# A two-block transformer kernel on one core: block 2's memory products moved into block 1's layer norms, its position table made by one product, its mixer's norm factor applied at the projections' evictions

## The chip, the core and the metric

The kernel runs on one core of a Trainium2 chip. Its time is the device time of one execution, in microseconds (us), and the number that counts is the median over the runs. The engines are TensorE (PE in the profile), VectorE (DVE), ScalarE (ACT), GpSimd (POOL) and SyncE (SP), which here only issues transfers. Each engine goes through its own instructions in order and waits on semaphores for the others.

## The reference, cut to what matters

Sequence 256, width 1024. Block 1 has two layers, each a hybrid mixer, a layer norm, a feed-forward part (dense SwiGLU in layer 0, eight experts in layer 1) and a layer norm. Block 2 has one layer, and only it changes:

```python
x = x + 0.5 * swiglu_ffn(rms_norm(x, ffn1_norm), ...)            # FFN 1
h = rms_norm(x, mix_norm)
q_a, k_a, v_a, q_i, k_i, w_i, u_s, q_m, gates = split(h @ w_in)  # 19 projections
bias = rel_bias[t5_bucket(sel - t)]                              # 32 buckets, 8 heads
mem_kv = rms_norm(mem, mem_norm) @ w_mem_kv                      # 256x1024 @ 1024x512
m_k, m_v = split(mem_kv)
... sparse attention, S5 states, memory attention, gates, w_out, FFN 2
```

`mem` is an input of its own: `mem_kv` and the position table depend on nothing that block 1 computes. An RMS factor is one number per token (row), so it may be applied after a product with the weights as well as before.

## The kernel before

Everything is one program, written out in order for each engine (blocks for `sync`, `gpsimd`, `tensor`, `scalar`, `vector`); no scheduler moves anything. The stages follow each other: mixer 0, layer norm 0, dense FFN, layer norm 1, mixer 1, layer norm 2, router and experts, layer norm 3, FFN 1 of block 2, preparation for block 2's mixer, that mixer, FFN 2.

**The ring.** All weights pass through a ring of six 1 MB places in SBUF (`ring_data`, class `Ring`, L155). SP issues load n in two halves as soon as PE has finished with n + 1 - 6 loads, which it tells by the semaphore `weights_used` (L170). The loads are numbered in the order of use: per mixer 14 projections and four parts of `w_out` (`MIX_LOADS` = 18), per dense FFN 33, then the experts.

**Split weights.** In the FFNs and experts each weight load is split by ACT (`high`, `e_high`: a rounded copy) and DVE (`low`, `e_low`: what is left), and PE multiplies the parts. At the end of each mixer, ACT and DVE split the first two loads of what comes next; on DVE these two come ahead of the residual adds (L2390 to 2398), and on ACT ahead of the norm's square root.

**A layer norm stretch.** After the last product of a mixer, DVE makes four residual adds with statistics (L2398), ACT a square root, DVE four normalizing operations, PE turns x (L889), and ACT and DVE evict it. PE has nothing else to do in between.

**Preparation (L1375 to L1400 of PE).** After FFN 1 PE turns the normalized memory (L874), multiplies it with `w_mem_kv` (two loads, L1384, 32 products 256 wide), makes the position table head by head (L1391: eight products 512 wide with the head's bias row repeated over 128 columns, each evicted by ACT and stored to DRAM by POOL), turns the S5 blocks (L1397, L1398), and turns the normalized x (L874), which ACT and DVE evict with `mix_norm`. Then the 19 projections start (L1413 to L1424). DVE normalizes x between (L2579), ACT squares it. The squares and the scaling of `mem` itself run in FFN 1 on ACT and DVE.

Of the kernel before, what the change touches and what calls it, by code (L numbers as in the profile page):

```python
# [10 lines left out]
ALU = mybir.AluOpType  # L11
# [38 lines left out]
FFN_LOADS, MOE_LOADS = 3 * FFN_CHUNKS, 3 * MOE_CHUNKS  # L50
LEVELS = 6
# [11 lines left out]
N_MEM = N_FFN1 + FFN_LOADS  # L63
N_PROJ2 = N_MEM + 2
# [6 lines left out]
R2_LDT, R2_FFN1, R2_MIX, R2_MEM, R2_FFN2, R2_LRE, R2_LIM, R2_D, ROWS2 = 0, 8, 16, 24, 32, 40, 48, 56, 58  # L71
# [49 lines left out]
def constant_offsets():  # L121
# [9 lines left out]
    ("lambda_inverse", "mk_sumsq", "mk_normed", "heads_sumsq", "heads_normed", "keys_chosen", "states_ready"),  # L131
    ("relb_ready", "angle_reduced", "blocks_ready", "powers_ready"),
    ("dt_ready", "unit_act", "mk_std", "mkT_act", "heads_std", "ys_ready"),
    ("router_psum", "place_psum", "bc_psum", "mkT_psum", "y_psum"),
# [113 lines left out]
PARAMS = {"pcol": (DEPTH, P), "hpar": (DEPTH, 24), "nrmw": (DEPTH, HD), "cln": (DEPTH, 2, CW), "router": (DT, E)}  # L248
# [6 lines left out]
def small_parameters(v):  # L255
# [13 lines left out]
    parts.append(v["moe_router"][0].reshape(DT, P, E).transpose(1, 0, 2).reshape(P, DT * E))  # L269
    return np.ascontiguousarray(np.concatenate(parts, 1), dtype=np.float32)  # L270
# [7 lines left out]
def two_block_kernel(nc, a, out):  # L278

    CO, CONST_W = constant_offsets()  # L280
    with ExitStack() as ctx:
# [59 lines left out]
        pcol, hpar, nrmw, cln, router_sb = (param(k) for k in PARAMS)  # L341
# [66 lines left out]
        sq, forget = ar(6, T), ar(T)  # L408
        fs, fp, fpT = ([ar(3 * P) for _ in range(2)] for _ in range(3))
        kend, vb = ar(TT, GW), ar(TT, GW)  # L410
        norm12, beta1, beta2, qscale, qsquare = ar(TT, 2 * H), ar(TT, H), ar(TT, H), ar(TT, H), ar(TT, H)
# [45 lines left out]
        ring2 = Ring(ring_data, [sem(f"loaded2_{i}") for i in range(RING)], sem("weights2_used"), sem("weights2_hi"), sem("weights2_lo"), (2 * MIX_LOADS + FFN_LOADS) % RING)  # L457
# [7 lines left out]
        tstage = bu.rearrange("p a b c -> p (a b c)").rearrange("p (h c) -> p h c", h=AH)  # L465
# [11 lines left out]
        qiT, kiT, kaT = ar(2, T), ar(T), ar(T)  # L477
        kva, kd = ar(TT, P), ar(TT, P)
        uT = ar(2, T)
        mkT = ar(2, T)  # L480
        at_bT = ar.at
        bT, cT = ar(2, 2, P), ar(2, 2, P)
        mkv = cln.rearrange("p a b c -> p (a b c)").rearrange("p (j c) -> p j c", j=TT)
        over = Area(at_q)
        relb, relb_bc = over(AH), over(AH, P)
# [5 lines left out]
        memx = arena[:, at_pw:at_pw + TT * D].rearrange("p (j d) -> p j d", j=TT)  # L491
        squares = arena[:, at_bT:at_bT + D]
        mk_sq = arena[:, 3 * D * TT:3 * D * TT + TT * T].rearrange("p (j c) -> p j c", j=TT)
        memT = arena[:, 4096:6144].rearrange("p (k t) -> p k t", k=DT)
# [4 lines left out]
        hi2 = [h[:, i, :] for h in (hi_gates, hi_bu) for i in range(3)]  # L499
        bufs2 = ffn_buffers(2, at_bu + 3 * 8 * FC, cln.rearrange("p a b c -> p (a b c)").rearrange("p (s j c) -> p s j c", s=2, j=TT))  # L500
# [4 lines left out]
        row1, row2 = sm(TT), sm(TT)  # L505
# [41 lines left out]
        n_moe = 2 * MIX_LOADS + FFN_LOADS  # L547
        dense_banks = [[4, 5], [6, 7]], [[0, 1], [2, 3]]
        ffn = Gated(sem, "ffn", ring, hi1, lo_slots, MIX_LOADS, 0, FFN_CHUNKS, 0, *dense_banks, (xT_hi, xT1_lo), bufs1)
# [16 lines left out]
        T_FFN, T_FFN1, T_MEM, T_MIX, T_MERGED, T_FFN2 = 2, 6, 7, 8, 9, 10  # L566
        SPLIT, MIXED = (T_FFN, T_FFN1, T_FFN2), (1, 4)

# [11 lines left out]
        def _(sp):  # L580
            sp.dma_start(actT[:, :, :], a["xT"]).then_inc(sem("xT_loaded"), 16)

            def mixer(l):
                n0 = (MIX_LOADS + FFN_LOADS) * l
                for m, (c, w, _) in enumerate(PROJ):
                    ring.load(sp, n0 + m, ring.slot(n0 + m)[:, 0:8 * w].rearrange("p (k c) -> p k c", k=DT), cols(a["w_in"][l], c, w))
                for m in range(OUT_LOADS):
                    n = n0 + len(PROJ) + m
                    ring.load(sp, n, ring.slot(n).rearrange("p (k c) -> p k c", k=DT), cols(a["w_out"][l], FC * m, FC))
# [269 lines left out]
        def _(pe):  # L859
# [41 lines left out]
            def mixer(l):  # L901
# [256 lines left out]
                for m in range(OUT_LOADS):  # L1158
                    out(m, (5, 6, 7), last=True)
# [1657 lines left out]
```

## Time and profile before

| what | us |
|---|---|
| runs before | 2364.22, 2367.36, 2368.49; median 2367.36 |
| span of the profiled execution | 2365.2 |
| PE busy in it | 2264.0 (96%) |
| end of FFN 1 to first projection of block 2 | 1861.6 to 1895.2 |
| layer norm 0, 1, 2 (PE's last product before to first product after) | 202.3 to 212.0, 404.9 to 415.8, 606.0 to 616.9 |

For the profiled execution only its span is given, from its first to its last instruction; it lies 2.2 us under the median of the runs. In a timeline row stand the start, the duration (from the first to the last of the instructions merged), engine, line, operation, tiles, count, and in brackets how long the engine stood idle before and what released it. A product of f32 stands in the trace as two instructions, a transpose as one.

### The profile page before, as it was taken

Reading aid. Unit: us, or ns where it says so; the run is one execution under the profiler, and the core shown is the slowest. Engines: PE = TensorE matmul, PEld = TensorE weight load, DVE = VectorE, ACT = ScalarE, POOL = GpSimd, SP = SyncE. Lnnn points to the kernel's source line nnn. Section 1 sums busy time; section 2 is a strip of 40 time slices with the busy share of each in tenths; the row PEclk is TensorE's granted clock in tenths of the full one; section 3 lists DMA queues with packets and bytes.
Section 4 is the critical chain, followed back from the end, with each engine's and each line's share of the span. In section 5 each row is a group of like instructions: output and inputs, shape, how many; then the busy total and the mean of one; then the engine's idle time right before and its main releaser. Section 6 shows DMA issues by size and latency. Waiting matters only on the chain.

```text
span 2365.2 us, 31984 instructions
## 1 busy us (share of the span) xinstructions
PE 2264.0 (96%) x12197; PEld 1864.0 (79%) x12197; DVE 1538.5 (65%) x1675; ACT 1159.3 (49%) x1159; POOL 146.1 (6%) x226
## 2 busy tenths in 40 slices
PE   8988998999799999999999999998899999999998
PEld 7977886887678888888888888886688788758886
DVE  3646444473688989898888989897655219434443
ACT  3133442313366777677677767676545211214442
POOL 1100000210200000000000000000570001000000
PEclk9999999999799999999999999999899999789999
DMA  8224554421489999999999999999355444224552
GB/s 288 71 75 143 180 188 152 125 78 54 144 328 347 357 341 356 354 352 358 343 357 344 353 344 354 345 355 329 120 200 180 153 148 128 89 89 134 180 189 75
DMA packets 254773, 538.02 MB, mean 227 GB/s; under 512 B 17839, under 2 KB 146913, under 8 KB 254433
## 3 DMA queue, kind: packets, MB, share of 16 engines
q1 hardware_dynamic: 250960, 523.21, 63.1%
q0 software_dynamic: 3168, 9.86, 1.3%
q10 hardware_dynamic: 560, 3.79, 0.4%
q8 instruction: 58, 0.95, 0.2%
q14 instruction: 27, 0.21, 0.0%
HBM read 533.65 MB, written 3.15 MB: 227 GB/s over the span
## 4 chain that ended last, share of the span: by engine, by line
PE 92%; DVE 5%; ACT 1%; issue 1%; DMA 0%; DVEq 0%; SPq 0%; ACTq 0%
PE bank L1290 9%; PE bank L1289 9%; PE bank L1293 9%; PE bank L1164 8%; PE bank L1165 8%; PE bank L1166 8%; PE bank L920 5%; PE bank L1424 5%; PE bank L1309 4%; PE bank L1304 4%; PE bank L1305 4%; PE bank L1111 2%; PE bank L1264 1%; DVE arena L2278 1%; PE bank L1572 1%; PE bank L1277 1%
## 5 line engine op out<-in xcount | busy, mean ns | idle before, releaser
L2082 DVE TENSOR_TENSOR weights_lo<-ring_data,weights_hi 128x2048 fp32r<-128x2048 f32 x336 | 759.6, 2290 | 101.3 <-ACT weights_hi L1813 100.2
L1813 ACT ACTIVATE weights_hi<-ring_data 128x2048 fp32r<-128x2048 f32 x336 | 637.4, 1917 | 177.5 <-DMA ring_data<-in_moe_w 176.3
L1289 PE MATMUL bank<-weights_hi,xg_hi 128*128 128x512 f32 x896 | 357.2, 399 | 4.0 <-DVE arena L2483 2.6
L1290 PE MATMUL bank<-weights_hi,xg_lo 128*128 128x512 f32 x896 | 354.6, 396 | 0.0
L2077 DVE TENSOR_TENSOR weights_lo<-ring_data,weights_hi 128x2048 fp32r<-128x2048 f32 x99 | 229.3, 2345 | 56.3 <-ACT weights_hi L1622 56.3
L1293 PE MATMUL bank<-weights_lo,xg_hi 128*128 128x512 f32 x896 | 242.9, 393 | 0.0
L1597 ACT ACTIVATE arena<-bank 128x384 f32<-128x384 f32 (+5 forms) x152 | 74.8, 514 | 335.7 <-PE bank L1424 99.0
L1164 PE MATMUL bank<-weights_hi,xT_hi 128*128 128x512 f32 x528 | 213.3, 404 | 2.3 <-DVE xT_lo L2070 2.3
L1165 PE MATMUL bank<-weights_lo,xT_hi 128*128 128x512 f32 x528 | 209.7, 397 | 0.0
L1166 PE MATMUL bank<-weights_hi,xT_lo 128*128 128x512 f32 x528 | 209.3, 396 | 0.0
L1289 PEld LDWEIGHTS bank<-weights_hi,xg_hi 128*128 128x128 f32 x896 | 168.2, 188 | 42.9 <-issue 3.0
L1293 PEld LDWEIGHTS bank<-weights_lo,xg_hi 128*128 128x128 f32 x896 | 168.4, 188 | 40.1
L1290 PEld LDWEIGHTS bank<-weights_hi,xg_lo 128*128 128x128 f32 x896 | 168.7, 188 | 38.8
L1622 ACT ACTIVATE weights_hi<-ring_data 128x2048 fp32r<-128x2048 f32 x99 | 185.7, 1918 | 0.0
L1304 PE MATMUL bank<-weights_hi,hT_hi 128*128 128x512 f32 x448 | 177.8, 397 | 1.5 <-DVE hT_lo L2489 1.5
L1305 PE MATMUL bank<-weights_hi,hT_lo 128*128 128x512 f32 x448 | 175.7, 392 | 0.0
L920 PE MATMUL bank<-actT,ring_data 128*128 128x256 f32 x608 | 136.1, 383 | 0.0
L2098 DVE TENSOR_TENSOR hT_lo<-bank,hT_hi 128x256 fp32r<-128x256 f32 x66 | 25.0, 420 | 170.2 <-ACT hT_hi L1633 170.2
L1633 ACT ACTIVATE hT_hi<-bank 128x256 fp32r<-128x256 f32 x66 | 21.7, 381 | 219.3 <-PE bank L1185 219.3
L920 PEld LDWEIGHTS bank<-actT,ring_data 128*128 128x128 f32 x608 | 115.3, 191 | 16.8 <-issue 0.4
L1309 PE MATMUL bank<-weights_lo,hT_hi 128*128 128x512 f32 x448 | 123.1, 397 | 0.0
L1164 PEld LDWEIGHTS bank<-weights_hi,xT_hi 128*128 128x128 f32 x528 | 100.1, 190 | 25.6 <-DVE xT_lo L2070 2.9
(444 smaller groups left out, 3198.4 us busy)
## 6 DMA issues: line engine op xcount, KB each, us to landing
ring_data<-in_moe_w SPq DMA_DIRECT2D x672, 512.0 KB, 4.4
ring_data<-in_ffn_w_in SPq DMA_DIRECT2D x88, 512.0 KB, 4.7
ring_data<-in_w_in SPq DMA_DIRECT2D x70, 512.0 KB, 4.8
ring_data<-in_ffn_w SPq DMA_DIRECT2D x66, 512.0 KB, 4.1
ring_data<-in_ffn_w_out SPq DMA_DIRECT2D x44, 512.0 KB, 4.0
ring_data<-in_w_out SPq DMA_DIRECT2D x24, 512.0 KB, 4.4
ring_data<-in_w_in SPq DMA_DIRECT2D x8, 396.0 KB, 4.1
ring_data<-in_w_in SPq DMA_DIRECT2D x8, 390.0 KB, 5.4
```

The lines of the kernel that those rows point to most:

```text
L920: i = mm(bk(b, 2, T)[:, g], wt[:, k, P * g:P * g + P], actT[:, k, :], start=k == 0, stop=k == DT - 1)
L1164: mm(o, x_hi, w_hi, start=start, stop=False, **kw)
L1165: mm(o, x_hi, w_lo, start=False, stop=False, **kw)
L1166: return mm(o, x_lo, w_hi, start=False, stop=stop, **kw)
L1289: mm(o, xg_hi[:, k, :], e_hi(at)[:, r], start=k == 0, stop=False)
L1290: mm(o, xg_lo[:, k, :], e_hi(at)[:, r], start=False, stop=False)
L1293: i = mm(bank[2 * part + q][:, :], xg_hi[:, k, :], e_lo(at)[:, r], start=False, stop=k == DT - 1)
L1304: mm(o, ehT_hi[:, 2 * m + f, :], w_hi[:, f, cd], start=first and f == 0, stop=False)
L1305: mm(o, ehT_lo[:, 2 * m + f, :], w_hi[:, f, cd], start=False, stop=False)
L1813: nc.scalar.activation(e_hi(at), ring_data[:, e_slot(at), :], ACT.Copy).then_inc(ring.hi_done, 1)
L2077: v.tensor_tensor(f.lo_slot(f.n0 + at), w, f.hi_slot(f.n0 + at), ALU.subtract).then_inc(f.ring.lo_done, 1)
L2082: v.tensor_tensor(e_lo(at), ring_data[:, e_slot(at), :], e_hi(at), ALU.subtract).then_inc(ring.lo_done, 1)
```

## The change

- `w_mem_kv` is loaded in four quarters of 128 columns (0.5 MB each), each in a place of block 1's ring: one between mixer 0 and the dense FFN, one between that and mixer 1, two between mixer 1 and the experts. PE multiplies a quarter (`memory`: 16 products 128 wide) after the last product of mixer 0, of the dense FFN and of mixer 1, and after the router's product. ACT evicts each with the memory's RMS factor.
- `mem` comes in twice in the first microseconds, once as it is (for the squares) and once transposed by the host (`memT`), on ACT's queue behind `x`; ACT scales `memT` by `mem_norm` (eight copies) and squares `mem` (two) in mixer 0. Nothing of it is left in FFN 1.
- The position table comes from one product (8 x 512) ahead of layer norm 3's transposes, evicted once, and stored by one transfer that reads the eight rows 128 times.
- PE turns x itself after FFN 1, ACT and DVE evict it with `mix_norm`, and the row factor is applied at the evictions: per token tile on ACT (two instructions where one was), and for the three products that stand transposed by DVE, with the factors spread over the partitions by two small products (`spread_rows`). The S5 blocks are turned after the second projection.

Core of the diff:

```diff
+N_MIX = (0, MIX_LOADS + 1 + FFN_LOADS + 1)
+N_FFN = MIX_LOADS + 1
+N_KV = (MIX_LOADS, N_MIX[1] - 1, N_MIX[1] + MIX_LOADS, N_MIX[1] + MIX_LOADS + 1)
+N_MOE = N_KV[3] + 1
# SP
             mixer(0)
+            memory(0)
             dense(ffn, a["ffn_w1"][0], a["ffn_w3"][0], a["ffn_w2"][0])
+            memory(1)
             mixer(1)
+            memory(2)
+            memory(3)
# POOL
-            pool.dma_start(memx[:, :, :], a["mem_2"][0].rearrange("(j p) d -> p j d", p=P)).then_inc(sem("mem_loaded"), 16)
-            for h in range(AH):
-                pool.wait_ge(sem("toep_act"), h + 1)
-                pool.dma_start(toep[h], tstage[:, h, :]).then_inc(sem("toep_stored"), 16)
+            pool.wait_ge(sem("act_stage"), stage("toep_act"))
+            pool.dma_start(toep, bc(tstage[0:AH, :], 1, P)).then_inc(sem("toep_stored"), 16)
+            pool.wait_ge(sem("toep_stored"), 16)
+            pool.wait_ge(sem("x_fed"), TT)
# PE
+            def memory(u, b):
+                n = N_KV[u]
+                ring.arrived(pe, n)
+                if u == 0:
+                    pe.wait_ge(sem("mem_scaled"), DT)
+                wt = ring.slot(n)[:, 0:8 * P].rearrange("p (k c) -> p k c", k=DT)
+                for j in range(TT):
+                    for k in range(DT):
+                        i = mm(bk(b, TT, P)[:, j], memT[:, k, P * j:P * j + P], wt[:, k, :], start=k == 0, stop=k == DT - 1)
+                i.then_inc(ring.used, 1)
...
                 for m in range(OUT_LOADS):
                     out(m, (5, 6, 7), last=True)
+                memory(2 * l, 7)
                 transpose_halves(x, 2 * l)
...
                 i.then_inc(sem("pe_stage"), 1)
+                memory(3, 6)
                 pe.wait_ge(sem("sel_ready"), 1)
...
+                mm(bank[5][0:AH, :], relb[0:32, :], const("hot")[0:32, :], start=True, stop=True).then_inc(sem("pe_stage"), 1)
...
-                for m in range(3):
-                    project(m)
+                project(0)
+                spread_rows()
+                project(1)
+                turn_blocks()
+                project(2)
# ACT
+                    if l == 0 and m == 1:
+                        act.wait_ge(sem("mem_loaded"), 32)
+                        for k in range(DT):
+                            a_(memT[:, k, :], memT[:, k, :], ACT.Copy, "mem_scaled", scale=memg[:, k:k + 1])
...
+                act.wait_ge(sem("pe_stage"), stage("toep_psum"))
+                a_(tstage[0:AH, :], bank[5][0:AH, :], ACT.Copy, "act_stage")
...
+                    for j in range(TT):
+                        a_(dst[:, j], o[:, j], f, "proj2_act" if j == TT - 1 else "act_steps", scale=rowm[:, j:j + 1])
# DVE
-            xT_out(T_MEM, gain(R2_MEM), memT, (4, 5, 6, 7))
-            rms(2, x, hbuf)
-            prepare_more()
-            xT_out(T_MIX, gain(R2_MIX))
-            keys_norm()
+            xT_out(T_MIX, gain(R2_MIX), actT, (4, 5, 6, 7))
+            mixer_factor()
+            keys_norm()
+            dve.wait_ge(sem("act_stage"), stage("row_spread"))
+            projected(0)
+            projected(1)
+            prepare_more()
```

SP's queue where mixer 0 ends and the dense FFN begins, and where mixer 1 ends and the experts begin (L184 and L187 are the same line of `Ring.load`; x8 of `w_out` are the halves of four loads). Before:

```order
L184 DMA ring_data<-in_w_in 128x4x256 x6
L184 DMA ring_data<-in_w_out 128x4x256 x8
L184 DMA ring_data<-in_ffn_w 128x4x256 x4
...
L184 DMA ring_data<-in_w_in 128x4x256 x6
L184 DMA ring_data<-in_w_out 128x4x256 x8
L646 DMA ring_data<-in_moe_w 128x1024 x16
```

And now:

```order
L187 DMA ring_data<-in_w_in 128x4x256 x6
L187 DMA ring_data<-in_w_out 128x4x256 x8
L187 DMA ring_data<-in_w_mem_kv 128x4x128 x2
L187 DMA ring_data<-in_ffn_w 128x4x256 x4
...
L187 DMA ring_data<-in_w_in 128x4x256 x6
L187 DMA ring_data<-in_w_out 128x4x256 x8
L187 DMA ring_data<-in_w_mem_kv 128x4x128 x4
L670 DMA ring_data<-in_moe_w 128x1024 x16
```

One load of memory weights stands ahead of the dense FFN's first, two ahead of the experts' first.

PE where mixer 1 ends, layer norm 2 and the router (before: L1111 is `w_out`, L889 turns x, L1246 is the router, L1250 to L1254 rank the tokens, L1264 gathers):

```order
L1111 MATMUL bank<-ring_data,actT 128x256 x24
L889 MATMUL bank<-consts_sb,x 128x128 x16
L1246 MATMUL bank<-params,actT 128x8 x16
L1250 MATMUL bank<-small,consts_sb 128x8
L1251 MATMUL bank<-small,consts_sb 128x8
```

And now (L1141, L905, L1279, L1284, L1285 are the same lines; L926 is `memory`):

```order
L1141 MATMUL bank<-ring_data,actT 128x256 x24
L926 MATMUL bank<-ring_data,arena 128x128 x16
L905 MATMUL bank<-consts_sb,x 128x128 x16
L1279 MATMUL bank<-params,actT 128x8 x16
L926 MATMUL bank<-ring_data,arena 128x128 x16
L1284 MATMUL bank<-small,consts_sb 128x8
L1285 MATMUL bank<-small,consts_sb 128x8
```

A quarter stands ahead of the turn of x, another between the router and the ranking.

PE from FFN 1's end to the third projection, before:

```order
L874 MATMUL bank<-consts_sb,arena 128x128 x16
L1384 MATMUL bank<-ring_data,arena 128x256 x32
L1391 MATMUL bank<-consts_sb,arena 128x512 x8
L1397 MATMUL bank<-consts_sb,arena 128x128
L1398 MATMUL bank<-consts_sb,arena 128x128
...
L874 MATMUL bank<-consts_sb,lnp 128x128 x16
L1413 MATMUL bank<-actT,ring_data 128x256 x16
L1417 MATMUL bank<-actT,ring_data 64x256 x16
L1420 MATMUL bank<-ring_data,actT 128x4 x16
L1424 MATMUL bank<-ring_data,actT 128x256 x16
```

And now:

```order
L890 MATMUL bank<-consts_sb,x 128x128 x16
L1438 MATMUL bank<-actT,ring_data 128x256 x16
L1414 MATMUL bank<-consts_sb,small 128x128 x2
L1442 MATMUL bank<-actT,ring_data 64x256 x16
L1445 MATMUL bank<-ring_data,actT 128x4 x16
L1422 MATMUL bank<-consts_sb,arena 128x128
L1423 MATMUL bank<-consts_sb,arena 128x128
...
L1449 MATMUL bank<-ring_data,actT 128x256 x16
```

The turn of the memory, its products and the table are gone from here; the two spreading products and the turn of the blocks stand behind the first and the second projection.

## Rows read from the trace of the kernel before

**Rows 1.** The page: the span, and the chain that ended last by engine.
```profile
span 2365.2 us, 31984 instructions
...
PE 92%; DVE 5%; ACT 1%; issue 1%; DMA 0%; DVEq 0%; SPq 0%; ACTq 0%
```

**Rows 2.** Timeline of PE from FFN 1's end to the first projection.
```profile
1861.62 1.91 PE L874 MATMUL bank<-consts_sb,arena 128*128 128x128 f32 x16
1864.89 14.05 PE L1384 MATMUL bank<-ring_data,arena 128*128 128x256 f32 x64 [1.36 <-ACT arena L1597]
1878.88 9.24 PE L1391 MATMUL bank<-consts_sb,arena 32*128 32x512 f32 x16
...
1890.56 3.62 PE L874 MATMUL bank<-consts_sb,lnp 128*128 128x128 f32 x16
1895.20 7.14 PE L1413 MATMUL bank<-actT,ring_data 128*128 128x256 f32 x32 [1.02 <-ACT actT L1597]
```

**Rows 3.** Timeline of DVE, end of block 2's states.
```profile
2040.71 0.87 DVE L2700 SCALAR_TENSOR_TENSOR arena<-arena,params,bank 128x256 f32<-128x256 f32 x2 [13.49 <-PE bank L1475]
```

**Rows 4.** Timeline of DVE at the end of mixer 0 and of mixer 1.
```profile
197.86 0.68 DVE L2398 SCALAR_TENSOR_TENSOR x<-x,bank 128x512 f32<-128x512 f32 x1
...
202.34 0.69 DVE L2398 SCALAR_TENSOR_TENSOR x<-x,bank 128x512 f32<-128x512 f32 x1 [0.26 <-PE bank L1111]
...
597.12 4.49 DVE L2082 TENSOR_TENSOR weights_lo<-ring_data,weights_hi 128x2048 fp32r<-128x2048 f32 x2 [1.97 <-ACT weights_hi L1813]
601.53 0.68 DVE L2398 SCALAR_TENSOR_TENSOR x<-x,bank 128x512 f32<-128x512 f32 x1
```

**Rows 5.** SP's queue: the loads released by the parts of `w_out`.
```profile
194.74 0.94 SPq L184 DMA_DIRECT2D ring_data<-in_ffn_w  x2
598.23 0.81 SPq L646 DMA_DIRECT2D ring_data<-in_moe_w  x2
600.82 0.80 SPq L646 DMA_DIRECT2D ring_data<-in_moe_w  x2
```

**Rows 6.** Timeline: PE leaves a place (experts' first load); ACT waits for its next content.
```profile
640.16 1.07 PE L1293 MATMUL bank<-weights_lo,xg_hi 128*128 128x512 f32 x4
646.02 1.92 ACT L1813 ACTIVATE weights_hi<-ring_data 128x2048 fp32r<-128x2048 f32 x1 [1.39 <-DMA ring_data<-in_moe_w]
```

**Rows 7.** Timeline of PE, layer norm 2 to the gather.
```profile
616.91 6.96 PE L1246 MATMUL bank<-params,actT 128*128 128x8 f32 x32 [0.88 <-DVE actT L2057]
626.07 0.60 PE L1250 MATMUL bank<-small,consts_sb 128*128 128x8 f32 x2 [2.19 <-DVE small L2424]
631.25 5.54 PE L1264 MATMUL bank<-arena,x 128*128 128x128 f32 x32 [2.88 <-DVE arena L2458]
```

**Rows 8.** The chain: products after layer norm 1; a gather among the experts.
```profile
415.79 7.58 PE bank L918 x32
...
747.58 3.57 PE bank L1264 x32
```

**Rows 9.** The table by stretch: PE, PEld, DVE, ACT, POOL busy (count), granted clock, DMA share, GB/s.
```profile
405.00:410.00 5.00, 0.00 (x0) 0.00 (x0) 4.59 (x11) 0.20 (x1) 0.00 (x0) 0.96 0.40 107
416.00:420.00 4.00, 4.00 (x13) 4.00 (x14) 0.00 (x1) 0.00 (x0) 0.00 (x0) 0.53 0.46 152
1880.00:1890.00 10.00, 9.31 (x20) 3.57 (x20) 0.00 (x0) 4.78 (x8) 4.38 (x8) 0.71 0.82 288
```

**Rows 10.** Timeline of ACT ahead of FFN 1 (layer norm 3).
```profile
1666.34 0.21 ACT L1597 ACTIVATE small<-params 128x8 f32<-128x8 f32 x1 [4.86 <-DVE params L2593]
1666.45 3.01 ACT L1597 ACTIVATE xT_hi<-bank,params 128x256 fp32r<-128x256 f32 x8
```

**Rows 11.** Timeline of DVE in mixer 0, where it waits for PE.
```profile
64.46 0.56 DVE L2239 TENSOR_TENSOR arena<-bank,small 128x384 f32<-128x384 f32 x1 [3.84 <-PE bank L972]
```

**Rows 12.** The table by stretch (columns as in rows 9), mixer 0.
```profile
45.00:50.00 5.00, 5.00 (x25) 4.41 (x24) 0.78 (x2) 2.80 (x8) 0.00 (x0) 1.00 0.08 9
```

**Rows 13.** Groups of POOL's instructions, 1855 to 1990 us: busy, mean ns | idle before.
```profile
L841 POOL DMA_DIRECT2D toep<-arena x8 | 4.4, 547 | 126.0 <-ACT arena L1597 126.0
```

More of the change, by code:

```diff
@@ L589, in mixer, with memory @@
                     ring.load(sp, n, ring.slot(n).rearrange("p (k c) -> p k c", k=DT), cols(a["w_out"][l], FC * m, FC))
+            def memory(u):
+                n = N_KV[u]
+                ring.load(sp, n, ring.slot(n)[:, 0:8 * P].rearrange("p (k c) -> p k c", k=DT), cols(a["w_mem_kv_2"][0], P * u, P))
             def up(f, w1, w3, c, at, r):
@@ L667, in _ @@
             dense(ffn1, w[:, 0:FFN], w[:, FFN:2 * FFN], a["ffn1_w_out_2"][0])
-            for m in range(2):
-                ring2.load(sp, N_MEM + m, slots_of(N_MEM + m, DT), cols(a["w_mem_kv_2"][0], FC * m, FC))
             for m, (c, w, _) in enumerate(PROJ2):
@@ L1576, in _ @@
             dense(ffn, 0)
+            memory(1, 7)
             transpose_halves(x, 1)
@@ L1668, in norm_std, with memory_out @@
                 a_(std[:, 0:TT], mv[:, :, 1], ACT.Sqrt, "ln_std", bias=LN_EPS)
+            def memory_out(u, b):
+                act.wait_ge(ring.used, N_KV[u] + 1)
+                if u == 0:
+                    act.wait_ge(sem("dve_stage"), stage("mem_factor"))
+                for j in range(TT):
+                    a_(mkv[:, j, P * u:P * u + P], bk(b, TT, P)[:, j], ACT.Copy, "mem_kv", scale=mem_r[:, j:j + 1])
             def mixer(l):
-                n0 = (MIX_LOADS + FFN_LOADS) * l
+                n0 = N_MIX[l]
                 def project(m):
@@ L1730, in mixer @@
                     a_(sq[:, 2 * m:2 * m + 2, :], qkv[:, 2 * m:2 * m + 2, :], ACT.Square, "qk_squares")
+                if l == 0:
+                    for j in range(TT):
+                        a_(memsq, memx[:, j, :], ACT.Square, "act_stage", accum_out=mem_ss[:, j:j + 1])
+                        act.wait_ge(sem("act_stage"), stage("mem_sq0") + j)
                 project(5)
@@ L1734, in mixer @@
                 act.wait_ge(sem("gdn_psum"), 7 * l + 6)
+                if l == 0:
+                    a_(mem_r[:, :], mem_ss[:, :], ACT.Sqrt, "act_stage", scale=1.0 / D, bias=NORM_EPS)
                 a_(norm12[:, :, :], bk(2, TT, 2 * H), ACT.Sqrt, "gdn_act", bias=NORM_EPS)
@@ L1950, in branches @@
                 a_(mkT[:, :, :], bk(4, 2, T), ACT.Copy, "act_stage")
-                for m in range(3, 7):
+                for m in (3, 4, 6):
                     project(m)
@@ L2021, in _ @@
             norm_std(1)
+            memory_out(1, 7)
             xT_out(3)
@@ L2215, in mixer @@
                 dve.wait_ge(sem("gdn_act"), 7 * l + 6)
+                if l == 0:
+                    dve.wait_ge(sem("act_stage"), stage("mem_std"))
+                    v.reciprocal(mem_r[:, :], mem_r[:, :]).then_inc(sem("dve_stage"), 1)
                 st.do(v.reciprocal(norm12[:, :, :], norm12[:, :, :]))
```

201 lines of the change are left out of this document (94 added, 107 removed).

## Prediction

> **What bounds the kernel now.** I read the chain of waits first: 92% of it is PE, and DVE, ACT and the rest share 8% [rows 1]. So only what PE itself does, or what it stands still for, counts. Then I went through PE's timeline for the two kinds of place that the diff touches. Between FFN 1 and block 2's first projection PE is nearly always busy, with work that needs nothing from block 1: it turns the memory from 1861.62, multiplies it for 14.05 us from 1864.89, makes the position table for 9.24 us from 1878.88, turns the blocks and x, and only at 1895.20 starts projecting [rows 2]. In the layer norm stretches PE stands still and DVE is the chain. Last I read who releases DVE there: its first residual add starts straight behind the split of the next stage's first two loads (4.49 us for two, 601.53 behind them), and only the fourth waits, 0.26 us, for PE [rows 4]. So DVE has no slack at the ends of the mixers, and that decides much below.
>
> **Part 1: the preparation leaves PE's path.** What is left between FFN 1 and the first projection is one turn of x and its eviction. The same steps stand in the trace as the turn of the memory: sixteen transposes from 1861.62, the evictions, the next product at 1864.89 [rows 2]. That its second half must now wait for the last add into x changes little, since x is added while PE still multiplies; I take 1865.0. Against 1895.20 that is -30.2 us. Two things come back: the blocks' eight transposes (sixteen took 1.91 us at one clock and 3.62 at the other [rows 2], so 0.9 to 1.8, and 0.9 amid full-speed projections) and the two spreading products (four instructions of 128 columns; 32 took 3.57 [rows 8], so 0.45). With a gap or so 1.5 us. Net -28.7. Bounds: if both run slow and PE waits for an eviction here and there, -26; if nothing comes back, -30.2. The row factor: ACT has two instructions for each projection where it had one, DVE three more, but each projection keeps PE for some 7 us (7.14 [rows 2]), and PE asks for a bank only four projections later. The factor itself (square, root, reciprocal, spreading) runs beside the first projection. DVE's chain of states has 13.49 us in which it waits at its end [rows 3], so a start a microsecond later costs nothing.
>
> **Part 2: the ring loses places at the mixers' ends.** The four quarters are loads of the ring. With six places, load n starts when PE is through with load n - 5. Before, the dense FFN's first two loads were numbers 18 and 19 and hung on the uses 13 and 14 of mixer 0, projections both; the third hung on the first part of `w_out`, and that one was issued at 194.74 [rows 5]. Now a memory quarter is 18, so the FFN's second load is number 20 and hangs on the first part of `w_out`: it will be issued at 194.74. Before the experts two quarters stand, so both of their first loads wait, for the first and second parts: 598.23 and 600.82 [rows 5], where now two later loads start. How long from release to ACT's split? Among the experts PE leaves a place at 641.23 (640.16 + 1.07) and ACT starts on its next content at 646.02, having waited for the DMA: 4.8 us [rows 6].
> Mixer 0: ACT splits at 194.74 + about 4.8 = 199.6, rounded up to 199.8 for the longer `ffn` rows, ends 1.92 later [rows 6] at 201.7, DVE takes 2.25 (half of 4.49 [rows 4]) to 204.0, and only then starts the adds, which started at 197.86. The fourth add stood 4.48 behind the first, with 0.26 of waiting that is now gone: 208.2 against 202.34. **+5.8.**
> Mixer 1: the second load is issued at 600.82; ACT starts at 605.6 and ends at 607.5, DVE at 609.8 against 601.53. Less the 0.26 [rows 4], **+8.0.** Bounds of the two together: +11 if loads land in 3.5 us, +17 if each meets another transfer.
>
> **Part 3: the products themselves.** A quarter is 16 products of 128 columns, 32 instructions, like the gather: 3.57 us warm [rows 8]. Behind mixer 0, the dense FFN and mixer 1 PE stands idle for longer than that, in the first and third now for longer still: 0. The fourth stands between the router and the ranking. There the granted clock is the lower level: the gather of the same 32 instructions took 5.54 [rows 7], since the clock rose only on its way. PE is free at 623.87 (616.91 + 6.96) and is asked for the ranking at 626.07 [rows 7]: 5.5 us of product put that off by 3.3. If the clock is then up, the ten ranking instructions take half (about -1.1) and the gather 3.57 for 5.54 (-2.0). Sum **+0.3**; bounds +4.7 (6.9 us at 1.2 GHz as the router's 32 instructions, nothing won) and -1.
> Layer norm 1 is where the filled gap may pay. Before, PE was idle from 404.9, the granted clock read 0.96 over 405 to 410 and 0.53 over 416 to 420 [rows 9]: it fell to 1.2 GHz before the transposes and stayed there into the first projection, whose 32 instructions took 7.58 [rows 8]. With 3.6 us of products in the gap it may stay at 2.4 GHz: the last transposes 1.0 shorter, the projection about 1.9. The Trainium skill (TensorE: Matmul & The Clock Gate, section Part 1: The HAM clock gate) has it that the low clock is the resting state and that sustained work lifts it; by that rule alone the whole 2.9 would be won. The transposes are short and have pauses around them, so I take **-2.0**, with bounds -2.9 and 0.
>
> **Part 4: small things.** ACT must evict the table (512 columns; the eight evictions of 256 take 3.01 [rows 10], so at most 0.75) between the small exponential at 1666.34 and the eviction of x at 1666.45 [rows 10], which is the chain there: **+0.6** (0 to 0.8). In mixer 0 ACT gets eight scalings of 256 columns and two squares of 1024 (by the same 0.38 for 256, 3.0 + 3.0) and a root. ACT mostly waits for PE there, so perhaps 2.3 of the 6.2 reach the last short convolution on DVE, and DVE waits 3.84 us for PE just behind it [rows 11]: hidden; were none of it covered by ACT's own waits, 6.2 - 3.84 = 2.4 would show. The 2 MB of `mem` join a burst of transfers that has ended by 45 us (9 GB/s over the next five [rows 12]); a load of 1 MB among the experts takes about the 2.8 us by which PE asks for them, so 2 MB some 5.7. They queue behind `x` on ACT's queue, and I find PE waiting for no load of mixer 0 but its first: 0, at worst +5.7. FFN 1 loses `mem`'s squares and scaling, beside which PE never stood still: 0.
>
> **Sum.** -28.7 + 5.8 + 8.0 + 0.3 - 2.0 + 0.6 = -16.0. The span goes from 2365.2 [rows 1] to 2349.2; the median of the runs lay 2.2 above the profiled span, so 2351.4.
>
> **Rivals.**
> *The ring keeps up.* If the transfers were in time after all, both delays of part 2 vanish: 2351.4 - 13.8 = 2337.6. For it: every transfer before was early. Against: the issue times stand in the queue, and the fence of the order leaves no place free.
> *The products do not fit.* The change only moves them: four quarters at 3.57 are the 14.05 of before. If the three in the norms end late (their loads or bank 7 late), 3 x 3.57 = 10.7 comes back: 2362. For it: nothing in the rows; PE idles 5 us there.
> *The start pays.* The transfers of `mem` delay PE's fourth or fifth load, and ACT's extra work shows: +5.7, 2357. For it: the DMA engines are full until 45 us. Against: they queue last.
> *The table arrives late (slower).* One transfer now reads eight partitions 128 times, where eight (x8 [rows 13]) read 128 partitions each, 2.1 MB in all. The heads follow the states at 2040.71 [rows 3] and need the bias. Even if the transfer started only at FFN 1's end, 1861.6 [rows 2], it would have 179 us. The ten microseconds of the stores before moved 288 GB/s in all [rows 9]; a sixteenth of that, for a sixteenth of the partitions, is 18 GB/s, 117 us: in time. From 11.7 GB/s down it is late; at 9 GB/s it takes 233 us, the heads start 54 late, and the kernel takes 2405. The Trainium skill (DMA: Bandwidth & Descriptors, section Rules for kernel authors) says that an outermost dimension under 16 confines a transfer to at most that many engines, here 8 of 16. By that rule it takes twice its least time, 15 us as an estimate, and nothing waits; no row before shows such a transfer.
>
> **How the numbers follow.** Forecast 0.64 (2346 to 2356 by its bounds), ring keeps up 0.10, products do not fit 0.06, start pays 0.12, table late 0.05; 0.03 for no effect at all. The range takes in the start's case and, below, the better bounds of parts 1 to 3 (-30.2, +11, -1, -2.9, so 2342), with a little of the first rival: 2341 to 2361. A change of 0.2% (4.7 us) is what can be told: faster 0.91, same 0.04, slower 0.05.
>
> **What would show it.** First projection of block 2 about 3.3 us behind FFN 1's last product, where 33.6 were. The fourth residual add of mixer 0 about 5.8 later and of mixer 1 about 8.0 later than before, with ACT waiting for the DMA ahead of the split loads. The product behind the router at 5 to 7 us and the gather near 3.6. A granted clock above 0.9 from 410 to 420 or not settles the -2.0. I would be wrong if the adds start where they did, if PE waits for loads in the first 60 us, or if POOL's table or the row factor holds up a projection or a head.

## Result and the profile after

| | us, median (lowest to highest), runs | ratio to the kernel before, 95% |
|---|---|---|
| kernel before | 2367.93 (2361.64 to 2374.32), 6 | |
| changed kernel | 2348.87 (2344.28 to 2354.48), 6 | 0.9922 [0.9908, 0.9935] |

The time lies 2.5 us under the forecast of 2351.4. The stages show that this is no proof of its sum: two terms of more than 20 us each, of opposite sign, stand in none of its parts.

First the forecast's own places. PE's timeline around FFN 1's end, in the kernel before and in the changed one (start, length, engine, line, operation, shape, count, idle before):

```profile
1861.39 0.40 PE L1166 MATMUL bank<-weights_hi,hT_lo 128*128 128x512 f32 x1
```
```profile
1873.08 0.39 PE L1197 MATMUL bank<-weights_hi,hT_lo 128*128 128x512 f32 x1
1873.31 2.04 PE L890 MATMUL bank<-consts_sb,x 128*128 128x128 f32 x16
```

and the long pieces of the chain behind it:

```profile
1876.71 7.14 PE bank L1438 x32
1884.30 6.24 PE bank L1442 x32
```

The first projection starts 3.6 us behind the start of FFN 1's last product; before it was 33.8 (1895.20 in [rows 2] less 1861.39). Counted from the first turn, as the forecast did, it is 3.4 against 33.6. That is part 1 as foreseen. The chain through the end of mixer 1 is part 2:

```profile
591.95 5.46 PE bank L1141 x24
597.43 0.33 SPq L670
...
597.80 4.89 DMA ring_data<-in_moe_w
602.71 1.92 ACT weights_hi L1861
604.65 2.29 DVE weights_lo L2114
606.94 0.61 DVE x L2433
```

Before, the adds followed straight on splits whose loads had come in time [rows 4]. Now they wait for this: a part of `w_out` gives its place free, the experts' second load takes 4.89 us, ACT and DVE split it, and only then comes the first add, at 606.94. The last product of `w_out` had ended at 602.58. The chain behind layer norm 2, and the gather on PE's timeline:

```profile
621.88 6.96 PE bank L1279 x32
628.85 5.35 PE bank L926 x32
```
```profile
638.19 5.44 PE L1298 MATMUL bank<-arena,x 128*128 128x128 f32 x32 [2.98 <-DVE arena L2493]
```

The fourth memory quarter (L926) stands between router and ranking; the gather (L1298) is as slow as in [rows 7]. And layer norm 1 (beside [rows 8, 9]), in the kernel before and in the changed one:

```profile
410.22 1.97 PE L889 MATMUL bank<-consts_sb,x 128*128 128x128 f32 x8 [5.32 <-DVE x L2171]
413.00 1.97 PE L889 MATMUL bank<-consts_sb,x 128*128 128x128 f32 x8 [0.81 <-DVE x L2171]
```
```profile
406.81 1.09 PE L905 MATMUL bank<-consts_sb,x 128*128 128x128 f32 x8 [1.79 <-DVE x L2203]
409.58 1.09 PE L905 MATMUL bank<-consts_sb,x 128*128 128x128 f32 x8 [1.68 <-DVE x L2203]
411.51 5.61 PE L948 MATMUL bank<-ring_data,actT 128*128 128x198 f32 x32 [0.83 <-ACT actT L1626]
```

Both groups of transposes are shorter. But the second starts 2.8 us behind the first in both kernels, since it waits for DVE's next normalized half: what the first group gains is not on the path, what the second gains is.

Now what the forecast had not. **FFN 1** took 192.4 us before and takes 214.7. The chain has one long piece there that is no product, a weight load of 35.69 us. ACT's timeline shows 31.47 us of waiting for the load before it (that one took 42.7 us from issue to landing), and POOL's the table's store that precedes both:

```profile
1747.18 1.20 POOL L857 DMA_DIRECT2D toep<-arena  x1
```
```profile
1755.91 4.52 SPq L187
1760.62 35.69 DMA ring_data<-in_ffn_w_out
```
```profile
1751.06 1.92 ACT L1651 ACTIVATE weights_hi<-ring_data 128x2048 fp32r<-128x2048 f32 x1
...
1793.78 1.91 ACT L1651 ACTIVATE weights_hi<-ring_data 128x2048 fp32r<-128x2048 f32 x1 [31.47 <-DMA ring_data<-in_ffn_w_in]
```

The table's store and its landing in the list of DMA issues (KB, median us from issue to landing), and the queues' share of the 16 DMA engines from 1755 to 1800 us:

```profile
toep<-arena POOLq DMA_DIRECT2D x1, 2048.0 KB, 45.5
```
```profile
q0 software_dynamic: 445, 1.79, 38.7%
q1 hardware_dynamic: 3035, 4.07, 28.5%
```

q0 is the queue of the store, q1 that of the weights. The store moves at 46 GB/s (2.1 MB in 45.5 us) and the weights crawl with it. **Every product** also got shorter. Here are the first and the last of 71 gated products that follow each other in FFN 2, in the kernel before and in the changed one:

```profile
2216.68 0.39 PE L1165 MATMUL bank<-weights_lo,xT_hi 128*128 128x512 f32 x1
...
2232.95 0.39 PE L1166 MATMUL bank<-weights_hi,xT_lo 128*128 128x512 f32 x1
```
```profile
2216.31 0.39 PE L1196 MATMUL bank<-weights_lo,xT_hi 128*128 128x512 f32 x1
...
2232.20 0.40 PE L1197 MATMUL bank<-weights_hi,xT_lo 128*128 128x512 f32 x1
```

70 steps in 16.27 us are 232.4 ns each, 70 in 15.89 are 227.0, with the granted clock at 1.00 in both. The length of an instruction (0.39) doesn't tell it; the distance of the starts does. Some 6270 such distances stand in each trace: by this estimate 33 us, and no line of the diff touches these products.

### The profile page after: what moved, and what is told of

Its sections match the earlier page's. It is cut to its first block, busy times and chain, and to the rows that moved or that the text cites. A ratio compares the mean times of both kernels' runs of the same rounds, so it can differ in the third digit from the quotient of the medians.

```text
span 2345.3 us, 32058 instructions
## 1 busy us (share of the span) xinstructions
PE 2221.3 (95%) x12235; PEld 1858.0 (79%) x12235; DVE 1537.6 (66%) x1670; ACT 1159.9 (49%) x1175; POOL 139.7 (6%) x216
## 4 chain that ended last, share of the span: by engine, by line
PE 87%; DVE 6%; DMA 3%; ACT 2%; issue 1%; SPq 0%; DVEq 0%; ACTq 0%
PE bank L1323 8%; PE bank L1324 8%; PE bank L1327 8%; PE bank L1195 7%; PE bank L1197 7%; PE bank L1196 7%; PE bank L950 5%; PE bank L1449 5%; PE bank L1338 4%; PE bank L1339 4%; PE bank L1343 4%; PE bank L1141 2%; DMA ring_data<-in_ffn_w_out 2%; PE bank L1298 1%; DVE arena L2313 1%
## 5 line engine op out<-in xcount | busy, mean ns | idle before, releaser
L1626 ACT ACTIVATE arena<-bank 128x384 f32<-128x384 f32 (+9 forms) x127 | 60.3, 499 | 202.7 <-PE bank L950 80.6
```

## Experiments

All ratios are to runs of the kernel before on the same chip. A figure in ns is the mean distance between the starts of neighbouring 512-column products, over all those of a trace that follow each other without a gap (under 300 ns; some 6270).

**1. The address.** The change adds eight floats a partition (`memg`) to `params`, and everything allocated behind it moves up by 32 bytes: the arena, which holds `weights_hi`, starts at byte 117888 before and 117920 now; `ring_data` stays at 31904. (`weights_lo` lies in `ring_data` and `xT_hi` in `actT`; the expectation below counts both to the arena, which is wrong.) The kernel before with nothing but this shift:

```diff
+        pad = sb("pad", [P, 8])
         headg = sb("headg", [P, 4, HD])
```

> The kernel before, with eight unused floats a partition (32 bytes) laid after the parameters, which is where the change lays the eight of mem_norm_2: ring_data, x, actT and params keep their addresses, headg, small and the whole arena (weights_hi, weights_lo, xT_hi, the hidden buffers) move up by 32 bytes. In the two traces at hand the 512-column products of all stages stand 232.5 ns apart before and 227.1 ns after, 5616 of them, some 30 us in all, and no term of the prediction has it. Theory A (the address of the arena sets the pitch): this kernel has 227 ns, and runs 25 to 32 us faster than the kernel before, 2335 to 2343 us, ratio about 0.988. Theory B (the pitch belongs to the chip or to the execution that was profiled): the pitch may come out either way, but the time is that of the kernel before, 2362 to 2372 us, ratio 0.998 to 1.002. Theory C (something else of the change, its instructions or its queues, sets the pitch): 232 ns and 2362 to 2372 us.

Measured: 2338.40 us, ratio 0.9885 [0.9863, 0.9907], 227.1 ns. The same 71 products:

```profile
2206.74 0.39 PE L1166 MATMUL bank<-weights_lo,xT_hi 128*128 128x512 f32 x1
...
2222.63 0.39 PE L1167 MATMUL bank<-weights_hi,xT_lo 128*128 128x512 f32 x1
```

Theory A. 32 unused bytes make the old kernel faster than the change makes it. The counterpart, the same pad in the changed kernel:

> The changed kernel with 32 unused bytes after the parameters, so that the arena lies at 0 modulo 64 as in the kernel before, and ring_data at 32. Theory A (the address gave the changed kernel its 227 ns, and the change itself, with its table store, costs time): 232.5 ns between 512-column products and 27 to 29 us slower than the changed kernel, 2374 to 2379 us, slower than the kernel before by 0.3 to 0.6%. Theory B (the changed kernel's own edits also set the pitch): 227 ns and 2345 to 2352 us.

Measured: 2377.12 us, ratio 1.0049 [1.0035, 1.0064], 232.1 ns: theory A. At the addresses of before, the change costs 0.5%.

**2. Which address.** `before_ring32` has the pad ahead of `ring_data`, `before_both32` has one there and one behind `params`.

> The kernel before, with eight unused floats a partition (32 bytes) laid ahead of ring_data, so that ring_data (with weights_lo in it), x, actT (with xT_hi in it), params and the arena (weights_hi, the hidden buffers) all move up by 32 bytes. Addresses of the compiled programs, modulo 64: kernel before ring_data 32, arena 0, 232.5 ns between 512-column products; changed kernel and before_plus32 ring_data 32, arena 32, 227 ns; here ring_data 0, arena 32. Theory H1 (the arena's own address counts, 32 modulo 64 is the fast one): 227 ns and 2334 to 2343 us. Theory H2 (the fast state is that in which the arena and ring_data agree modulo 64): 232.5 ns and 2362 to 2372 us. Theory H3 (each operand that a product reads has its share): between the two, about 229 to 231 ns and 2345 to 2360 us.

> The kernel before, with 32 unused bytes ahead of ring_data and 32 more after the parameters: modulo 64 ring_data lies at 0 and the arena at 0. H1 (the arena at 32 is fast, at 0 slow): 232.5 ns between 512-column products, 2362 to 2372 us. H2 (agreement of the two is fast): 227 ns, 2334 to 2343 us. H3 (0 modulo 64 is slow for each operand by itself): slower than the kernel before, 235 ns or more and 2380 us or more.

Measured: 2366.10 us, 1.0002 [0.9992, 1.0012], 232.4 ns; and 2339.02 us, 0.9886 [0.9868, 0.9904], 227.2 ns. H2: not where the arena lies but whether it agrees with `ring_data`. Two more, on the version with both amendments (experiments 3 and 4: 2310.49 us, 227.1 ns). `act_apart` has pads behind `ring_data` and behind `params`; `arena_plus64` has 16 floats behind `params`.

> The version with both amendments (table_16_splits), with 32 unused bytes behind ring_data and 32 more behind the parameters: modulo 64 ring_data (weights_lo) lies at 32, x, actT (xT_hi, xg_hi, xg_lo) at 0, the arena (weights_hi, hT_hi, hT_lo) at 32. Theory W (what counts is that the two parts of the weights, which TensorE streams in turn, agree modulo 64): 227 ns between 512-column products and 2310 us, within 3. Theory X (what counts is that the streamed weights and the loaded operand agree): the products with xT_hi, xg_hi and xg_lo as the loaded operand, about two thirds of them, take 232 ns, the others 227: 15 to 20 us slower, 2325 to 2331 us. Theory V (neither; other engines' accesses to x or actT): a slowdown with a pitch that is the same in both kinds of products.

> The version with both amendments (table_16_splits), with 64 unused bytes after the parameters: ring_data, x and actT stay, the arena moves up by 64 bytes. Modulo 64 all three still lie at 32; modulo 128 ring_data, x and actT lie at 32 and the arena at 96, as the arena and ring_data did in act_apart, which took 29 us more and where besides x and actT lay 32 bytes off. Theory 64 (agreement modulo 64 is enough, and act_apart was slow through x and actT): 227 ns between 512-column products and 2308 to 2313 us. Theory 128 (the agreement must hold modulo 128 or more, and act_apart was slow through the arena, x and actT having no part): 232 ns and 2336 to 2343 us.

Measured: 2339.80 us, 0.9879 [0.9862, 0.9897], 232.1 ns; and 2335.00 us, 0.9870 [0.9854, 0.9887], 231.0 ns. Theory W falls in its stated form, since ring and arena agreed modulo 64 in the first and it was slow; the second, nearest to theory 128, shows why: 64 bytes apart is slow too. All together, addresses modulo 128:

| kernel | ring_data | x, actT | arena | ns |
|---|---|---|---|---|
| before | 32 | 32 | 0 | 232.4 |
| before_ring32 | 64 | 64 | 32 | 232.4 |
| after_plus32 | 32 | 32 | 64 | 232.1 |
| act_apart | 32 | 64 | 96 | 232.1 |
| arena_plus64 | 32 | 32 | 96 | 231.0 |
| before_plus32, changed | 32 | 32 | 32 | 227.1, 227.1 |
| before_both32 | 64 | 64 | 64 | 227.2 |

The products that read only arena and ring (`hT` with `weights`) slow down like those with `xT` from `actT`. Open: the exact modulus (in every fast layout the arena starts 86016 bytes, 21 times 4096, behind `ring_data`, so 128 and any power of two up to 4096 fit), whether `actT` has a share of its own (the experts took 1017.9 us in `act_apart`, 1012.5 in `arena_plus64`, one trace each), and the mechanism.

**3. The table's store.** `table_16` stores the rows 16 times instead of 128; `table_128` keeps the 2 MB and their moment but reads them from all partitions.

```diff
-            pool.dma_start(toep, bc(tstage[0:AH, :], 1, P))
+            pool.dma_start(toep, bc(tstage[0:AH, :], 1, 16))
...
-                src = bass.AP(..., offset=first, ap=[[511, P], [P * 512, AH], [1, w]])
-                pool.dma_start(bias[:, :, o:o + w], src)
+                for p in range(0, P, 16):
+                    src = bass.AP(..., offset=first - p, ap=[[511, 16], [16 * 512, AH], [1, w]])
+                    pool.dma_start(bias[p:p + 16, :, o:o + w], src)
# table_128 instead of it
+            pool.dma_start(toep.rearrange("h p c -> p h c"), bc(const("hot")[:, 0:512], 1, AH))
```

> The changed kernel, but the position table is stored 16 times instead of 128 (256 KB instead of 2 MB, from the same 8 partitions), and the bias is read from it in 16 transfers of 16 partitions each, 8 for each of its two parts, instead of 2 transfers. Theory A (the store's 2 MB from 8 partitions held up the weights of FFN 1: its landing took 45.5 us, and the loads behind it 35.7 us): the store lands in about 6 us, the longest wait for a weight load in FFN 1 falls under 8 us, FFN 1 goes from 214.7 back to about 190 us, and the kernel is 18 to 24 us faster than the changed one, about 2327 us, ratio to the kernel before 0.983. The 16 reads cost POOL 16 issues of 0.9 us beside the projections and nothing on the path. Theory B (FFN 1 was slow for another reason, such as the clock that fell to 0.5 by itself or POOL's power steps on the shared port): FFN 1 stays at 210 to 215 us and the time at 2345 to 2352.

> The changed kernel, but the 2 MB that are stored as the table are taken from a constant that lies on all 128 partitions, at the same moment and to the same addresses; the position table's values are thereby left out of the scores. Theory A1 (it is the 8 source partitions that make the store slow and hold up other transfers): the store lands in 10 to 15 us, FFN 1 loses at most 6 us to it and takes 190 to 198 us, the kernel is 15 to 22 us faster than the changed one, 2327 to 2334 us. Theory A2 (it is the 2 MB themselves, whose time the weights share): FFN 1 streams 24 MB in some 190 us and has little to spare, so 2 MB more at 300 GB/s cost it 7 us or more whatever the source, and a landing of 40 us or more and 210 to 215 us for FFN 1 would say that the source's partitions do not matter: 2345 to 2352 us.

Measured: 2326.99 us, 0.9832 [0.9810, 0.9854], FFN 1 188.9 us; and 2325.56 us, 0.9822 [0.9799, 0.9844], FFN 1 188.9 us. The landings, of `table_16` and of `table_128`:

```profile
toep<-arena POOLq DMA_DIRECT2D x1, 256.0 KB, 7.3
```
```profile
toep<-consts_sb POOLq DMA_DIRECT2D x1, 2048.0 KB, 9.2
```

The store's queue in 50 us around the store, in the changed kernel (1745 to 1795) and in `table_128` (1750 to 1800): packets, MB, share of the 16 DMA engines' time.

```profile
q0 software_dynamic: 1040, 2.10, 41.2%
```
```profile
q0 software_dynamic: 528, 2.10, 12.4%
```

So A, and A1 in the main: the same bytes to the same place take 9.2 us from 128 partitions and 45.5 from eight, and only the latter stop the weights. By the two shares the same bytes held the engines for 330 us of engine time against 99, and 330 in 45.5 us is some 7 engines of 16 at a time (estimates from these lines). `table_128` changed two things at once, though: the number of source partitions and the outermost dimension of the transfer, from eight rows to 128. How much belongs to each was not separated.

I had allowed the 128-partition store up to 6 us; it cost nothing that shows. The expectation's "24 MB in some 190 us and has little to spare" is wrong: FFN 1 has 33 loads of 1 MB, and the trace of the kernel before shows 177 GB/s in it, where the experts get 351. There was room for 2 MB.

**4. The splits ahead of the adds.**

```diff
# DVE (ACT's e_high of mixer 1 moves in the same way)
-                for at in range(2):
-                    if l == 0:
-                        low(ffn, at)
-                    else:
-                        e_low(at, FFN_LOADS + at + 1)
                 if l == 0:
+                    low(ffn, 0)
...
                     split_xT(T_FFN, xT1_lo)
+                    low(ffn, 1)
                 else:
                     xT_out(3 * l + 2)
+                    for at in range(2):
+                        e_low(at, FFN_LOADS + at + 1)
```

> The changed kernel, but in mixer 0 VectorE subtracts the low part of the second split weight block after the layer norm and its transposes' evictions, instead of ahead of the residual adds, and in mixer 1 ScalarE and VectorE split the first two expert blocks after the layer norm's evictions. Theory A (the adds waited for a split whose load came late, the ring being one place longer): the adds start at the eviction of the first w_out product, the first transposes come 5 to 6 us earlier in mixer 0 and 7 to 9 us earlier in mixer 1, and the kernel is 11 to 15 us faster than the changed one, about 2336 us, ratio to the kernel before 0.9865. Theory B (the adds would be late anyway, since the memory products hold TensorE and the load itself is late): under 3 us, 2346 to 2351 us. In between if the splits that now come late hold up the first gated product: then TensorE waits for lo_done at the start of FFN 0 by up to 2.3 us.

Measured: 2334.17 us, 0.9875 [0.9852, 0.9899]. DVE at mixer 0's end:

```profile
191.88 0.68 DVE L2430 SCALAR_TENSOR_TENSOR x<-x,bank 128x512 f32<-128x512 f32 x1
...
198.56 0.69 DVE L2430 SCALAR_TENSOR_TENSOR x<-x,bank 128x512 f32<-128x512 f32 x1 [1.11 <-PE bank L1141]
```

Theory A: the adds follow the products again, the stretches are back at 5.3 and 10.9 us (table below), 14 us by the traces and 11 by the medians' ratios. The later split has a small price: once in FFN 0 TensorE now waits, 1.05 us, for banks that DVE zeroes only behind it.

**5. Both.**

> The changed kernel with both amendments, the table stored 16 times instead of 128 and the splits behind the layer norms. If the two are independent, their gains on the changed kernel add: 2348.9 less 22 less 14.7, 2312 us, ratio to the kernel before 0.977 to 0.979. If earlier starts only move the wait to the weight loads (FFN 0's and the experts' loads follow ring places that come free at the same time as before), less: 2318 us or more.

Measured: 2310.49 us (2308.33 to 2310.62), 0.9764 [0.9751, 0.9776]. The gains add (2312 expected).

**6. The clock in layer norm 1.**

```diff
-                    for k in range(DT):
+                    for k in ((0,) if u == 1 else range(DT)):
...
```

> The version with both amendments (table_16_splits), but of the 16 products of each token tile that stand in layer norm 1's gap (8 each, 128 columns), only the first of each tile is left: 2 products instead of 16 in all, so block 2's second memory quarter is not computed. Theory A (the 3.7 us of products in that gap keep the clock at 2.4 GHz, and that pays for mixer 1's first products): the granted clock falls behind the gap as in the kernel before, the transposes take 1.97 us instead of 1.09, the first projection 7.6 instead of 5.6 us, and the kernel is 2 to 4 us slower than table_16_splits (2312 to 2315 us). Theory B (the products are merely hidden and the clock's gain comes from elsewhere): transposes 1.09, projection 5.6 us, and 2310 us within 1.

Measured: 2312.46 us (2308.40 to 2316.66), 0.9764 [0.9749, 0.9779]: no difference that can be told. But all traces together speak:

```profile
404.85 1.97 PE L906 MATMUL bank<-consts_sb,x 128*128 128x128 f32 x8 [0.80 <-DVE x L2205]
407.65 7.15 PE L949 MATMUL bank<-ring_data,actT 128*128 128x198 f32 x32 [0.83 <-issue]
```

In the five traces whose gap is empty (before, its three shifted forms, this one) both groups of transposes take 1.97 us and the projection 7.15 to 8.23. In the nine with products there, the first transposes always take 1.09, the second 1.09 in three, and the projection 7.0 to 8.5 in eight; 5.61 came in one, the changed kernel's. The products keep 2.4 GHz across the first pause; where it falls then differs from execution to execution. And since the second group starts 2.8 us behind the first in either case, only its own shortening counts. From FFN 0's last product to mixer 1's first it takes 10.1 us in the three traces where the second group is short, 10.5 in one where it is half short (1.56), and 10.9 in all the others, products or none. So theory A's clock came, but its gain in this version is about 1 us at the most.

**7. The fourth quarter moved.** Its products of tile 0 stand ahead of layer norm 2's first transposes, those of tile 1 between the two groups.

```diff
+                for q in range(2):
+                    if l:
+                        memory(3, 6, (q,))
+                    pe.wait_ge(sem("ln_done"), 4 * l + q + 1)
...
-                memory(3, 6)
                 pe.wait_ge(sem("sel_ready"), 1)
```

> The version with both amendments (table_16_splits), but the fourth memory quarter leaves its place behind the router: its products of token tile 0 (1.9 us) stand between the third quarter's and the first transposes of layer norm 2, those of tile 1 between the two halves' transposes, where TensorE waits 1.8 and 1.7 us; ScalarE's evictions of it move with it. Theory A (TensorE, filled, keeps 2.4 GHz through the router): the router's 32 products take 3.5 us instead of 6.96, the ranking comes 3 us sooner behind them, together 5 to 7 us faster, 2304 us. Theory B (the clock falls at the router's 8-column products in any case): only the ranking's 3 us, less up to 0.5 us by which the transposes come later: 2307 to 2309 us. Theory C (the quarter was hidden behind the router): 2310 us or more.

Measured: 2307.42 us (2303.82 to 2309.95), 0.9738 [0.9723, 0.9754], the fastest version. PE:

```profile
603.18 1.95 PE L927 MATMUL bank<-ring_data,arena 128*128 128x128 f32 x16
605.03 1.09 PE L906 MATMUL bank<-consts_sb,x 128*128 128x128 f32 x8
606.99 5.50 PE L1286 MATMUL bank<-params,actT 128*128 128x8 f32 x32 [0.88 <-DVE actT L2096]
615.38 0.59 PE L1290 MATMUL bank<-small,consts_sb 128*128 128x8 f32 x2 [2.89 <-DVE small L2465]
```

Nearest to theory B: the router starts at 2.4 GHz and falls to 1.2 inside its own products (the granted clock is 1.00 to 608, 0.80 over the next us and 0.50 from 609; 5.50 us, neither 3.5 nor 6.96), and the ranking then runs at the low clock (0.59 a pair). From the last `w_out` product to the experts 31.6 us against 34.3. The medians lie 3 us apart, their intervals overlap, so by the times alone it is not shown to beat experiment 5; both beat the changed kernel.

## Right or wrong, step by step

Stretches on PE's timeline, us. They cover the whole span, so each column sums to it (to 0.1):

| stretch | before | after_plus32 | changed | three_early |
|---|---|---|---|---|
| mixer 0, to the end of its last `w_out` product | 202.3 | 198.5 | 197.7 | 197.9 |
| from there to the transposes | 5.3 | 11.2 | 11.2 | 5.3 |
| transposes and FFN 0 | 197.3 | 196.3 | 192.5 | 193.4 |
| FFN 0's end to mixer 1's first product | 10.9 | 10.5 | 10.1 | 10.9 |
| mixer 1, to the end of its last `w_out` product | 190.2 | 191.5 | 191.1 | 189.4 |
| from there to the router | 10.9 | 19.2 | 19.3 | 10.1 |
| router to the experts' first product | 21.3 | 25.2 | 23.2 | 21.5 |
| experts | 1017.3 | 1017.2 | 999.4 | 1000.3 |
| experts' end to FFN 1 | 13.5 | 14.0 | 14.0 | 14.0 |
| FFN 1, to the start of its last product | 192.4 | 215.6 | 214.7 | 188.1 |
| from there to the first projection | 33.8 | 3.6 | 3.6 | 3.6 |
| first projection to FFN 2 | 269.3 | 270.3 | 271.6 | 273.2 |
| FFN 2 and the end | 200.7 | 200.6 | 197.0 | 197.0 |

The second column has the addresses of before, so its difference is the change alone; the profiled spans are 2365.2 and 2373.8.

- **Part 1** (-28.7): right. -30.2 for the start. Of what comes back, the spreading products hold PE for 0.5 us and the blocks for 0.9 in the changed kernel's timeline, 1.4 where 1.5 stood. The stretch to FFN 2 can't test it: it takes 269.2 to 273.6 us in the traces of the kernel before and its shifted forms alone.
- **Part 2** (+5.8, +8.0): right, +5.9 and +8.3 (8.4 in the changed kernel), and experiment 4 takes them away again.
- **Part 3, router** (+0.3): mis-sized, +1.9 in the changed kernel and +3.9 in `after_plus32`. The product took 5.5 us as foreseen in the first (6.6 in the second), and the ranking behind it was fast. But I let the clock stay up longer: behind a pause of 2.98 us the gather took 5.44 (6.42), near the 5.54 of [rows 7] and not 3.57. The -2.0 that I credited it was not there.
- **Part 3, layer norm 1** (-2.0): mis-sized. The changed kernel's profile shows -0.8 up to the projection and -2.0 in it (5.61 for 7.58), together near the -2.9; the eight other traces with the products don't show the second, and the first only two of them in full. What recurs in all nine, 0.9 us of the first transposes, is not on the path. That the clock gate's rule (the Trainium skill, TensorE: Matmul & The Clock Gate, Part 1: The HAM clock gate) would give the 2.9 held for one execution of nine.
- **Part 4**: +0.5 for layer norm 3 where 0.6 stood. Mixer 0 ends between 197.7 and 203.0 us from trace to trace, whichever kernel, so ACT's scalings and squares there and the start's transfers can't be told from nothing. The rival that the transfers cost 5.7 was right that they delay others: the slowest of the first weight loads took 26.9 us to land, 21.8 before. But PE waits for a load only once in mixer 0, for the first, 8.2 us against 8.3 before.
- **FFN 1** (0): this step failed. "FFN 1 loses `mem`'s squares ..: 0" looked only at what left it. The store moves from the gap after FFN 1, where it was eight transfers from 128 partitions each, into FFN 1's stream as one from eight, and costs +23 (215.6 for 192.4; at the fast addresses 214.7 for the 188.9 of experiment 3). The rival *table late* had the transfer, and its rate better than feared (46 GB/s, not 18), but asked only when the bias arrives, not what its packets do to others. A loss of 5.7 for 2 MB, as I worked out for `mem`, would have been wrong too: it is the form of the transfer that matters, eight source rows or 128. The page I cited (the Trainium skill, DMA: Bandwidth & Descriptors, Rules for kernel authors) gave 15 us as an estimate, a third of the 45.5. Its limit of 8 engines agrees with the 7 of experiment 3; that a byte held its engine 3.3 times as long is not in it. Another of its pages comes near: SBUF — State Buffer, section Door 1: The DMA port swizzle, has partitions 0 to 7 behind two of 16 ports of 27.2 GB/s each, an estimate of 39 us for 2.1 MB. That other transfers stall meanwhile, this trace shows with the 35.69 us; no run here separates the ports from the engines.
- **The products' pace** (in no part): -28, by the changed kernel against `after_plus32`. "No effect" rested on the unspoken premise that unchanged code keeps its time.

At equal addresses the change costs 8.6 us by the spans and 11.6 (0.49%) by the runs, where -16.0 stood. Against the forecast that is 27.6 too many by the runs. The store's 23.3, 3.6 at the router and 2.0 at layer norm 1 (0.4 shorter there, and the projection behind it 0.4 longer, 8.02 us) are 28.9, and account for it. (The spans differ by less than the runs because mixer 0 came out 3.8 us shorter in the one trace.) The forecast time came out because 28 us of address outweighed 23 of the store and the terms of part 3. The mechanisms of parts 1 and 2 were right; the total was luck. The range has a slip besides: its lower end of 2342 is a span, and the median of the runs would be 2.2 above it.

## What to carry to other kernels

When a trace after a change shows unchanged instructions at a new pace, compare buffer addresses before telling a story, and price a change at equal addresses: here 32 bytes of padding were worth more than the edit. Price a transfer also by what shares the DMA engines while it runs, and before you store a broadcast from a handful of partitions while weights stream, measure it: here it took five times as long as from 128 and stopped the stream. A ring that gains a load shifts every later one by a place: put what waits for those loads behind the work that is ready.

## What the hardware showed unexpectedly

- 512-column products with the split weights in two buffers: 227 ns apart in the layouts where `ring_data`, `actT` and the arena agree modulo 128 bytes, 231.0 to 232.4 ns where the arena is 32 or 64 bytes off `ring_data`; 1.2% of the whole kernel.
- 2.1 MB stored from 8 partitions land in 45.5 us, from 128 (and in 128 rows) in 9.2; beside the first, weight loads of another queue took up to 42.7 us against a median of 4 to 5.
- In `three_early` the clock fell inside the router's products although TensorE had been at work at 2.4 GHz until 0.9 us before them: 5.50 us for what takes 6.96 at 1.2 GHz (one trace).
